# Modulation sums on TensorE: four column strips hold four column blocks over all k, and one transpose turns the rows

## The chip, the core and the metric

The kernel runs on one core of a Trainium2 chip. The metric is device time in microseconds of one execution. The core has five engines with their own instruction streams: TensorE (PE; its weight loads are listed as PEld), VectorE (DVE), ScalarE (ACT), GpSimd (POOL) and SyncE (SP, which here issues the weight transfers). They meet at semaphores only.

## The reference, cut to what matters

Two transformer blocks of 256 tokens and 1024 features. The first has two layers; each layer's norms, gates and shifts are set by a "modulation" vector, which comes from one conditioning vector for the latent stream and one for the context stream:

```python
sc, scc = jax.nn.silu(c), jax.nn.silu(c_ctx)          # c: (1, 1024), c_ctx: (1024,)
for i in range(2):
    m  = (sc  @ ada_w[i] + ada_b[i]).reshape(-1, 9, 1024)   # ada_w[i]: (1024, 9216)
    mc = (scc @ ada_w[i] + ada_b[i]).reshape(9, 1024)
    x = x + 0.5 * m[:, 2] * swiglu(modulate(x, norm_g[i, 0], m[:, 0], m[:, 1]), ...)
    ...
```

So the whole of `ada_w` (2 x 1024 x 9216 floats, 75.5 MB) is multiplied with two vectors. Everything else (five gated feed-forward layers, a state-space mixer, a pooling mixer, a second block with two mixers) is not touched by the change.

## The kernel before, in words

**Layout.** Features lie on the 128 partitions, tokens along the free axis: a stream `x` is [128, 8, 256]. A product with a weight matrix takes three TensorE passes per 128x128 block (lines 612 to 614, the helper `mm3`), because each operand is split in a high and a low part. Weights arrive in chunks of 1 MB, three slots deep: SP loads `raw`, ACT rounds it to the high part (line 1217), DVE subtracts for the low part (line 1649), and PE waits for that in `take`.

**Modulation.** The 9216 columns of a layer are taken 256 at a time: a slot `ada[i]` holds [128, 8, 256], k on partitions and in the middle index. Two slots, 512 columns, are a "pair" for this part of the kernel; there are 36 of them. The stationary operand is `scv[:, k, :]`, 128 x 32: column 0 is silu(c), column 1 silu(c_ctx), the other 30 are zero. With 32 stationary columns a matmul fills one of four column strips of the array, and writes 32 partitions of a PSUM bank.

- `ada_sums` (PE, lines 628 to 636): for each of the two slots and each k, one matmul of 256 moving columns into the strip `k % 4`. A strip thus holds the sum over two of the eight k, and the bank [128, 512] has four partial sums per column block, at rows 0, 1, 32, 33, 64, 65, 96 and 97. Operands are fp32, and each such matmul stands in the trace as two weight loads and two matmul records.
- `ada_copy` (DVE, line 1690) copies the bank to `ada_rows` in SBUF.
- `ada_turn` (PE, lines 638 to 644): four matmuls with `ada_rows` as stationary operand and the constant `strip_sum` (128 x 2) as moving operand add up the strips and put the columns on partitions: 2 results for each of 4 blocks.
- `ada_keep` (DVE, line 1695) adds the bias and stores into `mods_all`.

**Order.** Each engine's order is written out by hand. In a prologue four pairs run one after the other, sums, copy, turn, in banks 2 and 5 and with the results in bank 0; one DVE instruction (line 1778) then stores all of them. The other 32 pairs lie in the loops of the first four feed-forward layers (`ADA_LOOPS`, 10 + 10 + 10 + 2), one for each pass of `pair(j)`:

```python
hidden(g + 2, 0, None, j - 1)            # 48 passes of mm3 blocks, bank 0
ada_sums((0, 1), ..., 2)                 # bank 2
pe.wait_ge(S["h_done"], pairs + j)
down(g + 3, opens, False, j - 1)         # banks 4 to 7
ada_turn(m0 - 1 + j, 3, 0, 0)            # after a wait for mods_done; bank 3
hidden(g + 4, 1, None, j - 1)            # bank 1
```

DVE's order in the same pass: the product for `hidden`, one low part, `ada_copy`, one low part, `ada_keep`, one low part. POOL waits for `ada_done` and then issues the transfers of the next two slots (line 503), so they have almost a whole pass to land.

Of the kernel before, what the change touches and what calls it, by code (L numbers as in the profile page):

```python
# [34 lines left out]
P = 128  # L35
T = 256
TT = T // P
D = 1024
KB = D // P
# [29 lines left out]
ROT = 32  # L69
# [6 lines left out]
ADA_FIRST = 8  # L76
# [45 lines left out]
def shape_constants():  # L122
# [7 lines left out]
    causal = neg(l <= s)  # L130
# [20 lines left out]
    wide[:ROT, 2 * T + 32:] = rot  # L151
    strip_sum = (s % 32 == np.arange(2)[None, :]).astype(np.float32)
    f32 = np.concatenate([ident, mask_f, mask_b, causal, cmp_mask[0], cmp_mask[1], wide, strip_sum], 1)

# [18 lines left out]
def two_block_kernel(nc, a, out):  # L173

    ctx = ExitStack()
    with ctx:
# [20 lines left out]
        scratch = fixed("scratch", [P, KB, T])  # L197
        NCONST = P + 2 * T + P + 32 + 2 * T + 32 + ROT + 2
        consts = fixed("consts", [P, NCONST])
# [24 lines left out]
        ada += [nc.alloc_sbuf_tensor_at(f"ada{6 + i}", [P, KB, 256], F32, offset=u_at + 8 * i * KIB) for i in range(2)]  # L224
        ada_rows = [over(f"ada_rows{i}", [P, 512], (56 + 2 * i) * KIB) for i in range(2)]
        uc_hi = over("uc_hi", [P, KB, T], 16 * KIB, F32R)
# [91 lines left out]
        rot = consts[0:ROT, _o + 32:_o + 32 + ROT]  # L318
        strip_sum = consts[:, _o + 32 + ROT:_o + 34 + ROT]

# [288 lines left out]
        def _(pe):  # L609
# [18 lines left out]
            def ada_sums(slots, loads, bk):  # L628

                for n, slot in enumerate(slots):  # L630
                    pe.wait_ge(ada_in[slot], 16 * loads)
                    for k in range(KB):
                        strip = 32 * (k % 4)
                        m = pe.matmul(bank[bk][strip:strip + 32, 256 * n:256 * n + 256], scv[:, k, :],  # L634
                                      ada[slot][:, k, :], start=k < 4, stop=k >= 4)
                m.then_inc(S["ada_done"], 1)

            def ada_turn(pair, bk, at, buf):

                pe.wait_ge(S["ada_rows"], pair + 1)  # L640
                for blk in range(4):
                    m = pe.matmul(bank[bk][:, at + 2 * blk:at + 2 * blk + 2], ada_rows[buf][:, blk * P:(blk + 1) * P],  # L642
                                  strip_sum, start=True, stop=True)
                m.then_inc(S["ada_turned"], 1)

# [114 lines left out]
            for m in range(ADA_FIRST // 2):  # L760
                if m >= 2:
                    pe.wait_ge(S["ada_rows"], m - 1)
                ada_sums((2 * m, 2 * m + 1), 1, (2, 5)[m % 2])
                ada_turn(m, 0, 8 * m, m % 2)
            pe.wait_ge(S["root_done"], 2)
# [871 lines left out]
        def _(ve):  # L1637
# [49 lines left out]
            def ada_copy(pair, bk, buf):  # L1687

                ve.wait_ge(S["ada_done"], pair + 1)
                ve.tensor_copy(ada_rows[buf][:, :], bank[bk][:, :]).then_inc(S["ada_rows"], 1)  # L1690

            def ada_keep(pair):

                ve.wait_ge(S["ada_turned"], pair + 1)
                ve.tensor_tensor(mods_all[:, bass.ds(4 * pair, 4), :],
                                 bank[3][:, 0:8].rearrange("p (b v) -> p b v", v=2),
                                 cols[:, bass.ds(4 * pair, 4)].unsqueeze(2).to_broadcast([P, 4, 2]), ALU.add)\
                    .then_inc(S["mods_done"], 2)
# [74 lines left out]
            for m in range(ADA_FIRST // 2):  # L1773
                if m >= 2:
# [3 lines left out]
            ve.tensor_tensor(mods_all[:, 0:2 * ADA_FIRST, :],  # L1778
                             bank[0][:, 0:4 * ADA_FIRST].rearrange("p (b v) -> p b v", v=2),
                             cols[:, 0:2 * ADA_FIRST].unsqueeze(2).to_broadcast([P, 2 * ADA_FIRST, 2]), ALU.add)\  # L1780
# [572 lines left out]
```

## Time and profile before

| | |
|---|---|
| three executions | 2394.72, 2405.93, 2409.69 us |
| median | 2405.93 us |
| profiled execution, span from first to last instruction | 2404.9 us |
| PE busy | 2210.8 us (92%) |
| DVE busy | 1349.1 us (56%) |
| ACT busy | 989.0 us (41%) |
| POOL busy | 182.7 us (8%) |

The profiled execution's span is 1.0 us below the median of the three executions; of what lies outside the span nothing is recorded. Matmul records overlap, so a busy time of PE is not the sum of its records: where `x32` stands behind a row, the time in the row is from the first start to the last end. Read a cost on PE as the distance between the starts of its neighbours.

### The profile page before, as it was taken

To read this page: it belongs to the slowest core of one execution; us is meant where nothing else is said; L and a number is where in the kernel's file an instruction comes from. 1 tells how busy PE (TensorE), PEld (TensorE's weight loads), DVE (VectorE), ACT (ScalarE), POOL (GpSimd) and SP (SyncE) were. 2 spreads that over 40 slices of the span, in tenths; PEclk is the share of its full clock that TensorE was granted. 3 is DMA by queue.
4 is the path that set the end of the run, shared out by engine and by line. 5 is a ranking of instruction groups with operands and counts; after the bars stand their busy time and mean duration, and the time that the engine had idled before them with its cause. 6 is when DMAs were issued, how large, how long until landed. Compare 5 with 4: busy or idle time off the path is not lost.

```text
span 2404.9 us, 40229 instructions
## 1 busy us (share of the span) xinstructions
PE 2210.8 (92%) x17317; PEld 2075.3 (86%) x17317; DVE 1349.1 (56%) x1632; ACT 989.0 (41%) x1113; POOL 182.7 (8%) x153
## 2 busy tenths in 40 slices
PE   3899999989998989999999899979999898799897
PEld 2799899989977888999899899969999688799867
DVE  2544454459779965444544654455765435776543
ACT  2433354433333644333434444345444434544522
POOL 1000000000010000000000000001310000230000
PEclk7999999999998889999999999989999799899878
DMA  9477767742222436777555445535434133344401
GB/s 314 141 265 261 245 224 259 260 161 90 88 88 88 141 105 228 262 262 244 176 176 185 131 140 185 182 99 164 125 122 129 48 119 110 123 125 120 144 1 53
DMA packets 270788, 383.79 MB, mean 160 GB/s; under 512 B 8441, under 2 KB 230727, under 8 KB 270679
## 3 DMA queue, kind: packets, MB, share of 16 engines
q1 hardware_dynamic: 246983, 293.59, 38.1%
q0 software_dynamic: 22288, 85.02, 10.4%
q10 hardware_dynamic: 1408, 3.59, 0.4%
q8 instruction: 85, 1.39, 0.2%
q14 instruction: 24, 0.20, 0.0%
HBM read 381.06 MB, written 1.11 MB: 159 GB/s over the span
## 4 chain that ended last, share of the span: by engine, by line
PE 79%; DVE 13%; ACT 4%; DMA 2%; issue 2%; POOL 0%; ACTq 0%; DVEq 0%; SPq 0%
PE bank L612 22%; PE bank L613 21%; PE bank L614 21%; DVE w_hl L1649 3%; PE bank L634 3%; PE bank L986 2%; PE bank L625 2%; ACT w_hl L1217 1%; PE bank L642 1%; DVE e_long L1950 1%; DVE e_long L1968 1%; DVE rstd L1659 1%; DVE conv_acc L1899 1%; PE bank L1033 1%; DMA ada<-in_ada_w 1%
## 5 line engine op out<-in xcount | busy, mean ns | idle before, releaser
L1649 DVE TENSOR_TENSOR w_hl<-raw,w_hl 128x2048 fp32r<-128x2048 f32 (+1 forms) x281 | 640.7, 2282 | 475.5 <-ACT w_hl L1217 475.3
L612 PE MATMUL bank<-u_hi,w_hl 128*128 128x256 f32 x2376 | 696.4, 293 | 28.2 <-DVE u_lo L1680 24.4
L613 PE MATMUL bank<-u_lo,w_hl 128*128 128x256 f32 x2376 | 684.4, 288 | 0.0
L614 PE MATMUL bank<-u_hi,w_hl 128*128 128x256 f32 x2376 | 683.8, 288 | 0.0
L1217 ACT ACTIVATE w_hl<-raw 128x2048 fp32r<-128x2048 f32 (+1 forms) x281 | 531.1, 1892 | 274.8 <-PE bank L614 252.4
L612 PEld LDWEIGHTS bank<-u_hi,w_hl 128*128 128x128 f32 x2376 | 467.1, 197 | 45.0 <-issue 35.0
L613 PEld LDWEIGHTS bank<-u_lo,w_hl 128*128 128x128 f32 x2376 | 468.8, 197 | 0.5 <-issue 0.5
L614 PEld LDWEIGHTS bank<-u_hi,w_hl 128*128 128x128 f32 x2376 | 468.1, 197 | 0.0
L612 PE MATMUL bank<-h_hi,w_hl 128*128 128x256 f32 x880 | 252.2, 287 | 11.6 <-DVE h_lo L1713 11.6
L613 PE MATMUL bank<-h_lo,w_hl 128*128 128x256 f32 x880 | 248.3, 282 | 0.0
L614 PE MATMUL bank<-h_hi,w_hl 128*128 128x256 f32 x880 | 248.2, 282 | 0.0
L612 PEld LDWEIGHTS bank<-h_hi,w_hl 128*128 128x128 f32 x880 | 167.4, 190 | 25.9 <-DVE h_lo L1713 13.1
L613 PEld LDWEIGHTS bank<-h_lo,w_hl 128*128 128x128 f32 x880 | 167.4, 190 | 0.0
L614 PEld LDWEIGHTS bank<-h_hi,w_hl 128*128 128x128 f32 x880 | 167.3, 190 | 0.0
L1265 ACT ACTIVATE h_hi<-h_full 128x512 fp32r<-128x512 f32 x55 | 34.8, 632 | 296.0 <-DVE h_full L1711 296.0
L612 PE MATMUL bank<-uc_hi,w_hl 128*128 128x256 f32 x520 | 149.1, 287 | 3.6 <-DVE uc_lo L1680 2.2
L613 PE MATMUL bank<-uc_lo,w_hl 128*128 128x256 f32 x520 | 147.1, 283 | 0.0
L614 PE MATMUL bank<-uc_hi,w_hl 128*128 128x256 f32 x520 | 146.9, 282 | 0.0
L612 PE MATMUL bank<-w_hl,u_hi 128*128 128x256 f32 (+1 forms) x368 | 111.8, 304 | 16.5 <-DVE w_hl L1649 11.7
L503 POOL DMA_DIRECT2D ada<-in_ada_w x72 | 63.4, 886 | 771.0 <-PE bank L634 659.7
L613 PE MATMUL bank<-w_hl,u_hi 128*128 128x256 f32 (+1 forms) x368 | 108.7, 295 | 0.0
L614 PE MATMUL bank<-w_hl,u_lo 128*128 128x256 f32 (+1 forms) x368 | 108.5, 295 | 0.0
(333 smaller groups left out, 3437.0 us busy)
## 6 DMA issues: line engine op xcount, KB each, us to landing
ada<-in_ada_w POOLq DMA_DIRECT2D x72, 1024.0 KB, 8.2
raw<-in_w_in SPq DMA_DIRECT2D x60, 1024.0 KB, 5.2
raw<-in_ffn_w_gate SPq DMA_DIRECT2D x55, 1024.0 KB, 7.2
raw<-in_ffn_w_up SPq DMA_DIRECT2D x55, 1024.0 KB, 5.3
raw<-in_ffn_w_down SPq DMA_DIRECT2D x55, 1024.0 KB, 5.0
raw<-in_ssd_w_in SPq DMA_DIRECT2D x20, 1024.0 KB, 5.3
raw<-in_w_out SPq DMA_DIRECT2D x16, 1024.0 KB, 5.2
raw<-in_ssd_w_out SPq DMA_DIRECT2D x8, 1024.0 KB, 5.2
```

The source lines that it names most:

```text
L503: pool.dma_start(ada[slot][:, :, :], src).then_inc(ada_in[slot], 16)
L612: pe.matmul(out_, wh, xh, start=start, stop=False, skip_group_check=True)
L613: pe.matmul(out_, wh, xl, start=False, stop=False, skip_group_check=True)
L614: return pe.matmul(out_, wl, xh, start=False, stop=stop, skip_group_check=True)
L625: m = pe.matmul(bank[bk][:, 0:T], ones[:, :], scratch[:, k, :], start=k == 0, stop=k == KB - 1)
L634: m = pe.matmul(bank[bk][strip:strip + 32, 256 * n:256 * n + 256], scv[:, k, :], ada[slot][:, k, :], start=k < 4, stop=k >= 4)
L642: m = pe.matmul(bank[bk][:, at + 2 * blk:at + 2 * blk + 2], ada_rows[buf][:, blk * P:(blk + 1) * P], strip_sum, start=True, stop=True)
L986: m = pe.matmul(bank[un // 4][:, (un % 4) * P:(un % 4 + 1) * P], ka[:, h, t], qa[:, h, t], start=True, stop=True)
L1033: pe.matmul(bank[4 + hp][:, :], vsw[:, br, 0, f], pt0[:, 2 * hp:2 * hp + 2, :], start=False, stop=False, skip_group_check=True)
L1217: nc.scalar.activation(whi[slot][:, 0:n], raw[slot][:, 0:n], ACT.Copy).then_inc(S["hi_done"], 1)
L1265: nc.scalar.activation(h_hi[:, :, :].rearrange("p k t -> p (k t)"), hf[:, :], ACT.Copy)\
L1649: ve.tensor_tensor(wlo[slot][:, 0:n], raw[slot][:, 0:n], whi[slot][:, 0:n].bitcast(F32), ALU.subtract)\
```

## The change

`ada_sums` now waits for both slots, and then runs over k outside and over four blocks of 128 columns inside. Block `blk` goes to strip `blk`, and accumulates there over all eight k. The bank then holds finished sums in 128 columns: row 32 b holds block b for the latent stream, row 32 b + 1 for the context stream. The copy takes 128 columns instead of 512. `ada_turn` is one transpose of [128, 128] against the identity, after which column 32 b + v is block b, vector v; `ada_keep` and the prologue's last store read those columns with a stride of 32. The constant `strip_sum` is gone, and the turned pairs of the prologue take 128 columns of bank 0 each.

```diff
             def ada_sums(slots, loads, bk):
-                for n, slot in enumerate(slots):
+                for slot in slots:
                     pe.wait_ge(ada_in[slot], 16 * loads)
-                    for k in range(KB):
-                        strip = 32 * (k % 4)
-                        m = pe.matmul(bank[bk][strip:strip + 32, 256 * n:256 * n + 256], scv[:, k, :],
-                                      ada[slot][:, k, :], start=k < 4, stop=k >= 4)
+                for k in range(KB):
+                    for blk in range(4):
+                        strip = 32 * blk
+                        m = pe.matmul(bank[bk][strip:strip + 32, 0:P], scv[:, k, :],
+                                      ada[slots[blk // 2]][:, k, (blk % 2) * P:(blk % 2 + 1) * P],
+                                      start=k == 0, stop=k == KB - 1)
                 m.then_inc(S["ada_done"], 1)

             def ada_turn(pair, bk, at, buf):
                 pe.wait_ge(S["ada_rows"], pair + 1)
-                for blk in range(4):
-                    m = pe.matmul(bank[bk][:, at + 2 * blk:at + 2 * blk + 2], ada_rows[buf][:, blk * P:(blk + 1) * P],
-                                  strip_sum, start=True, stop=True)
-                m.then_inc(S["ada_turned"], 1)
+                pe.transpose(bank[bk][:, at:at + P], ada_rows[buf][:, :], ident).then_inc(S["ada_turned"], 1)
...
-                ada_turn(m, 0, 8 * m, m % 2)
+                ada_turn(m, 0, P * m, m % 2)
...
-                ve.tensor_copy(ada_rows[buf][:, :], bank[bk][:, :]).then_inc(S["ada_rows"], 1)
+                ve.tensor_copy(ada_rows[buf][:, :], bank[bk][:, 0:P]).then_inc(S["ada_rows"], 1)
...
-                                 bank[3][:, 0:8].rearrange("p (b v) -> p b v", v=2),
+                                 bank[3][:, 0:P].rearrange("p (b v) -> p b v", v=32)[:, :, 0:2],
...
-                             bank[0][:, 0:4 * ADA_FIRST].rearrange("p (b v) -> p b v", v=2),
+                             bank[0][:, :].rearrange("p (b v) -> p b v", v=32)[:, :, 0:2],
```

The buffer `ada_rows` shrinks from [128, 512] to [128, 128], and the table of constants by two columns.

## Rows read from the trace of the kernel before

**Rows 1.** The page: busy time, and the chain that ended last.
```profile
PE 2210.8 (92%) x17317; PEld 2075.3 (86%) x17317; DVE 1349.1 (56%) x1632; ACT 989.0 (41%) x1113; POOL 182.7 (8%) x153
...
PE 79%; DVE 13%; ACT 4%; DMA 2%; issue 2%; POOL 0%; ACTq 0%; DVEq 0%; SPq 0%
```

**Rows 2.** Windows: span, busy PE, PEld, DVE, ACT, POOL; clock, DMA share, GB/s.
```profile
380.65:400.82 20.17, 20.17 (x186) 19.11 (x185) 9.02 (x7) 9.31 (x8) 1.77 (x2) 1.00 0.78 259
1404.03:1421.18 17.15, 17.15 (x146) 17.15 (x145) 8.26 (x5) 6.75 (x6) 0.00 (x0) 1.00 0.58 189
```

**Rows 3.** TensorE's waits from 307 to 520 us: total, times, longest.
```profile
PE bank L612 <- DVE h_lo L1713: 0.4, 1, 0.4
```

**Rows 4.** The turn and the copy: ns minimum/median/maximum; who waited for them (us, times).
```profile
L642 PE MATMUL bank<-consts,ada_rows x288: 165/251/374, 57.3 to 1204.3; 128*128 128x2 f32 x144
L1690 DVE COPY ada_rows<-bank x36: 683/693/693, 56.5 to 1198.0; 128x512 f32<-128x512 f32 x36
...
  DVE mods L1695: 128.4, 31
```

**Rows 5.** The same for the sums, line 634.
```profile
L634 PE MATMUL bank<-ada,silu_c x1152: 378/379/637, 29.0 to 1197.5; 128*32 128x256 f32 x192
```

**Rows 6.** Timeline around one group of sums: start, us, engine, line.
```profile
385.37 0.28 PE L614 MATMUL bank<-u_hi,w_hl 128*128 128x256 f32 x1
...
385.58 1.93 PE L634 MATMUL bank<-ada,silu_c 128*32 128x256 f32 x32
...
387.44 0.38 PE L612 MATMUL bank<-h_hi,w_hl 128*128 128x256 f32 x1
```

**Rows 7.** Records of line 634 running in four short stretches: PE, PEld.
```profile
385.57:385.64 0.07, 0.06 (x4) 0.07 (x8) 1.00 0.00 0
385.74:385.80 0.06, 0.06 (x4) 0.00 (x0) 1.00 0.00 0
385.81:385.86 0.05, 0.05 (x8) 0.04 (x4) 1.00 0.00 0
...
386.02:386.07 0.05, 0.05 (x8) 0.04 (x4) 1.00 0.00 0
```

**Rows 8.** Timeline around one turn of the rows.
```profile
393.12 0.28 PE L614 MATMUL bank<-h_hi,w_hl 128*128 128x256 f32 x1
...
393.24 0.95 PE L642 MATMUL bank<-consts,ada_rows 128*128 128x2 f32 x8
393.44 1.91 ACT L1217 ACTIVATE w_hl<-raw 128x2048 fp32r<-128x2048 f32 x1 [5.36 <-PE bank L614]
...
394.05 0.37 PE L612 MATMUL bank<-u_hi,w_hl 128*128 128x256 f32 x1
```

**Rows 9.** Timeline around eight 128x128 transposes, line 807.
```profile
612.70 0.28 PE L614 MATMUL bank<-uc_hi,w_hl 128*128 128x256 f32 x1
612.82 1.04 PE L807 MATMUL bank<-consts,x_silu 128*128 128x128 f32 x8
613.61 0.36 PE L612 MATMUL bank<-u_hi,w_hl 128*128 128x256 f32 x1
```

**Rows 10.** The chain that ended last, in the prologue: start, us, what.
```profile
57.25 1.87 PE bank L642 x8
59.12 3.62 PE bank L634 x32
...
63.51 1.05 PE bank L642 x8
...
66.56 0.70 DVE ada_rows L1690
```

**Rows 11.** Window of the prologue, columns as in rows 2.
```profile
59.00:62.70 3.70, 3.69 (x33) 1.39 (x33) 0.00 (x0) 0.00 (x0) 0.00 (x0) 0.50 0.69 242
```

**Rows 12.** VectorE's copies from PSUM, 512 and 62 columns.
```profile
L1760 DVE COPY cols<-bank 128x512 f32<-128x512 f32 x1 | 0.7, 691 | 16.0 <-PE bank L742 16.0
...
L1761 DVE COPY cols<-bank 128x62 f32<-128x62 f32 x1 | 0.2, 211 | 0.0
```

More of the change, by code:

```diff
@@ L151, in shape_constants @@
     wide[:ROT, 2 * T + 32:] = rot
-    strip_sum = (s % 32 == np.arange(2)[None, :]).astype(np.float32)
-    f32 = np.concatenate([ident, mask_f, mask_b, causal, cmp_mask[0], cmp_mask[1], wide, strip_sum], 1)
+    f32 = np.concatenate([ident, mask_f, mask_b, causal, cmp_mask[0], cmp_mask[1], wide], 1)
     levels = np.zeros((P, len(LEVELS), P), np.float32)
@@ L197, in two_block_kernel @@
         scratch = fixed("scratch", [P, KB, T])
-        NCONST = P + 2 * T + P + 32 + 2 * T + 32 + ROT + 2
+        NCONST = P + 2 * T + P + 32 + 2 * T + 32 + ROT
         consts = fixed("consts", [P, NCONST])
@@ L224, in two_block_kernel @@
         ada += [nc.alloc_sbuf_tensor_at(f"ada{6 + i}", [P, KB, 256], F32, offset=u_at + 8 * i * KIB) for i in range(2)]
-        ada_rows = [over(f"ada_rows{i}", [P, 512], (56 + 2 * i) * KIB) for i in range(2)]
+        ada_rows = [over(f"ada_rows{i}", [P, P], (56 + 2 * i) * KIB) for i in range(2)]
         uc_hi = over("uc_hi", [P, KB, T], 16 * KIB, F32R)
@@ L318, in two_block_kernel @@
         rot = consts[0:ROT, _o + 32:_o + 32 + ROT]
-        strip_sum = consts[:, _o + 32 + ROT:_o + 34 + ROT]
         def col(name):
```

## The prediction, made before the change was run

> **What bounds the kernel now.** I read the page first: TensorE is busy for 92% of the span and makes up 79% of the chain that ended last [rows 1]. That is an average, so next I looked at the stretch that the change touches, one pass of a feed-forward loop with modulation work in it, against a pass without. TensorE is busy for the whole of both: 20.17 of 20.17 us and 17.15 of 17.15 us, at the full granted clock (1.00, which is 2.4 GHz), with VectorE at 9.02 us, ScalarE at 9.31 us and the DMA engines at 0.78 [rows 2]. The waits say the same: over some ten such passes TensorE waited 0.4 us in all [rows 3]. So in the loops each microsecond taken off TensorE's stream comes off the total, and time taken off the copies on VectorE is worth nothing. The two kinds of pass differ by 20.17 - 17.15 = 3.02 us, which is what one group of sums and one turn cost today.
>
> In the prologue it is different. Four groups run one after the other, and TensorE and VectorE take turns on the chain: turn 1.87 us, sums 3.62, copy 0.70, turn 1.05, sums, copy, and so on [rows 10]. There the copies count too.
>
> **Sums in the loops.** Now: 16 matmuls, 32 records of 256 columns. From the start of the last ordinary matmul before them to the first behind them it is 387.44 - 385.37 = 2.07 us [rows 6]. Inside, the weight loads come in rounds of four, at 385.57 (eight, the first two rounds), then four at 385.81 and four at 386.02, and none between [rows 7]: four strips stream together, a round takes about 0.215 us, and eight rounds make 1.72. The last record starts 1.93 - 0.38 = 1.55 us after the first [rows 5, 6]. After: 32 matmuls, 64 records of 128 columns, in 16 rounds. The columns streamed in each strip stay the same (8 x 256 = 16 x 128, a strip). A round of 128 fp32 columns should take half of 0.215, 0.108; the transposes of line 807, also 128 fp32 columns, are (1.04 - 0.28)/7 = 0.109 apart, with 0.28 for the length of one record, taken from their neighbour [rows 9]. I take 0.109: 16 x 0.109 = 1.744, against 1.72 now, so **+0.02 us** per group.
>
> For this the extra instructions must be free. Twice as many weight loads have to pass: four in 0.109 us. Eight ran within the first 0.07 us [rows 7], so the loading itself has room. What no row shows is twice the number of instructions fed at that rate for a whole group: 64 weight loads and 64 matmuls in 1.74 us. Between ends: the fastest that rows show is this burst (below the need, so nothing lost), and the slowest reading is that 32 pairs in 1.72 us, 0.054 us a pair, is already what the engine can be fed; then 64 pairs take 3.44, +1.72 us a group. I take the first end, since the rounds of four with gaps between them show an engine that waits for its columns, not for instructions.
>
> A rule speaks against the change here. The Trainium skill ("TensorEngine Tiling (Array Packing)", Instruction Overhead) gives each matmul an overhead of some 60 cycles and warns against taking the tiling factor from a dimension that is already small; as an estimate from that page, 32 further records at 60 cycles of 2.4 GHz, 25 ns, would add 0.8 us a group, as much as the turn gives back. The trace disagrees as far as it goes: weight loads of neighbouring strips start within hundredths of a microsecond of each other [rows 7]. It is rival B.
>
> **Turn in the loops.** Now: four matmuls, eight records, each with a weight load of 128 columns [rows 4], from 393.12 to 394.05, 0.93 us [rows 8]. After: one transpose. Eight transposes in the same kind of stream take 612.70 to 613.61, 0.91 us [rows 9]; one takes 0.91 - 7 x 0.109 = 0.14 by the same reckoning. So **-0.79 us** per turn. Bounds: nothing shows one transpose alone inside the stream; were its place as long as a whole record, 0.28, the gain would be 0.65; more than 0.93 - 0.12 (an ordinary step) = 0.81 cannot be gained.
>
> Per pass that is -0.77 us, and a pass should take 19.40. There are 36 copies in all [rows 4], of which 4 are the prologue's, so 32 passes: 32 x 0.77 = **-24.6 us**.
>
> **What could be late next there.** ScalarE waits 5.36 us for TensorE before it may round the next chunk [rows 8], so weights are ready well ahead. DMA goes from 0.78 to 0.81 at unchanged bytes. The added wait, for the second slot before the first matmul, costs nothing in the loops: POOL issues both transfers after the last group, a pass of some 20 us earlier. Behind it on TensorE stands the `down` product; it would show as a wait of line 634. VectorE's store waits for the turn (128.4 us in 31 waits [rows 4]), and the low part queued behind it is not wanted for a further two products; the turn ends earlier, so this only eases. The copy, 0.69 to about 0.28, is hidden.
>
> **Prologue.** Copies: 512 columns take 0.691 us and 62 take 0.211 [rows 12], 1.07 ns a column above a fixed part, so 128 take 0.28: -0.41 each, four times: -1.6. Turns at full clock: 1.05 [rows 10] becomes one load and one record, some 0.05 + 0.28 = 0.33: -0.72, three times: -2.2. The first turn runs at half clock, 1.87 [rows 10], and the twice as long transpose takes 0.5 to 0.66: -1.3. The sums keep their column counts: +0.02 each. Against it, the granted clock was 0.50 (1.2 GHz) in the stretch of the second group, whose sums took 3.62 us, while the third took 66.56 - 63.51 - 1.05 = 2.0 us, so at 2.4 GHz [rows 10, 11]. If the clock rises at the same moment while the work comes some 2 us earlier, half of the third group runs at the low clock: +0.9. Sum **-4.2 us**. Bounds: -5.1 without that, -1.6 if two groups run at 1.2 GHz (2 x 1.7 = 3.4 given back). Behind the prologue VectorE's norm sets the pace, and it moves up whole.
>
> **Sum.** -24.6 - 4.2 = -28.8 us: the profiled span of 2404.9 becomes 2376. The span stands 1.0 us under the median of three, 2405.93, so I forecast 2377.
>
> **Rivals.**
> *A, instructions bind (slower).* The group keeps 0.054 us a pair. +1.72 a group, times 36 = +62, less the turns and copies, 32 x 0.79 + 4.2 = 29.5: +32, **2438 us**. It decides at the point where the group grows by more than 0.79, that is where 64 pairs take over 2.5 us, 0.039 us a pair. For it: no row shows a pair faster than that over more than a few rounds. Against it: the gaps between rounds [rows 7]. The Trainium skill ("TensorE: Matmul & The Clock Gate", Wait — 56ns, not 53.3ns?) says that in one mode of decoding a matmul costs the sequencer about 62 ns; by that the group would be near 4 us, an estimate, and this case the outcome. The trace has 0.054 us a pair today, already below it. Chance 0.10.
> *B, a small part of each record is not shared.* An ordinary matmul of 256 columns steps 0.12 where its 256 streamed columns would take half of 0.215, 0.108: 0.012 over. If 32 more records each add that, a group costs +0.4 and the loops give 32 x 0.37 = 12, with the prologue's 4 less 4 x 0.4, 2.6, that is 14.5: **2391**. At 0.024 a record the loops gain nothing and the prologue 1: 2405. The row against it is that of the four loads in 0.05 us [rows 7]. The overhead that the Trainium skill names in "TensorEngine Tiling (Array Packing)" would be this case. Chance 0.12.
> *C, the loops gain nothing.* TensorE's shorter stream turns into a wait (for h, for the low part, for the slots), and only the prologue's 4 us stay: **2402**. Only 0.4 us of waiting now [rows 3] speaks against it. The same time comes out if the strips stop overlapping a little at each change of k. Chance 0.08.
> *Forecast:* 0.70.
>
> **How the numbers follow.** A measurement of this kernel tells about 1% from no change: its three executions span 15 us. Faster by over 1% means below 2381.9, 5 us above my forecast; with that scatter I give the forecast's cases 0.8 to pass it, 0.70 x 0.8 = 0.56, and a little from B: 0.58. Slower: A, 0.10. Within 1%: 0.32. The range takes in the forecast with its bounds (the prologue's -1.6, the turn's 0.65, each side's scatter of some 10 us), B and most of C: 2364 to 2402. A is left outside.
>
> **What would show it.** In the changed kernel: a pass of 19.4 us; line 634 with x64 a group, lasting 1.93 us, and weight loads in rounds every 0.11 us; the turn one record, with 0.14 us taken from its stretch; copies near 0.28 us; the prologue 4 us shorter. Wrong would be a group over 2.5 us without rounds (A), one of 2.3 us (B), or a new wait of TensorE in the passes (C).

## The result, and the profile after

The changed kernel takes **2367.44 us** (median of four executions, 2360.87 to 2368.37), beside 2403.81 us (median of four) for the kernel before: ratio 0.985, 95% interval 0.9831 to 0.9868. That is 36 us, or 1.5%, less. I had forecast 2377 us, 28.8 us less. The profiled execution has a span of 2366.4 us against 2404.9, so 38.5 us less.

The page of the kernel after, with the rows that answer to [rows 1]: 900 more records on TensorE, yet 27 us less busy time. The chain keeps its shares. This only says that nothing else took over.

```profile
PE 2183.9 (92%) x18217; PEld 2076.5 (88%) x18217; DVE 1338.3 (57%) x1632; ACT 988.8 (42%) x1113; POOL 182.7 (8%) x153
...
PE 79%; DVE 13%; ACT 4%; DMA 2%; issue 2%; POOL 0%; ACTq 0%; DVEq 0%; SPq 0%
```

**The pass.** The window of one pass with modulation work (columns as in [rows 2]): 19.40 us in place of 20.17, with TensorE busy throughout and at full clock, and no wait added. It is what the prediction named, within a hundredth. A pass without modulation work has become 0.06 us longer (17.21 between the starts of neighbouring passes, read at ScalarE's line 1262, against 17.15 in [rows 2]), which nothing in the change explains at first sight.

```profile
370.28:389.68 19.40, 19.40 (x212) 19.07 (x211) 8.72 (x8) 9.31 (x7) 1.92 (x3) 1.00 0.77 270
```

**The sums.** TensorE's timeline around one group (line 633 now, with x64; [rows 6] before): from the last ordinary matmul ahead of it to the first behind it, 387.78 - 385.68 = 2.10 us, against 2.07.

```profile
385.68 0.28 PE L612 MATMUL bank<-u_hi,w_hl 128*128 128x256 f32 x1
385.89 1.95 PE L633 MATMUL bank<-ada,silu_c 128*32 128x128 f32 x64
387.78 0.38 PE L610 MATMUL bank<-h_hi,w_hl 128*128 128x256 f32 x1
```

**The turn.** The same around one turn (line 641; [rows 8] before): one load, one record, and the next ordinary matmul starts 0.03 us behind it. From 374.06 to 374.21 is 0.15 us; from 393.12 to 394.05 it was 0.93.

```profile
374.06 0.28 PE L612 MATMUL bank<-h_hi,w_hl 128*128 128x256 f32 x1
...
374.18 0.27 PE L641 MATMUL bank<-consts,ada_rows 128*128 128x128 f32 x1
...
374.21 0.36 PE L610 MATMUL bank<-u_hi,w_hl 128*128 128x256 f32 x1
```

**The copy and who waits** (durations in ns, minimum/median/maximum, as in [rows 4]). The copy takes 292 ns in place of 693, and VectorE's wait for the turn falls from 128.4 us to 111.1. Both are hidden in the loops.

```profile
L1687 DVE COPY ada_rows<-bank x36: 283/292/293, 53.4 to 1164.0; 128x128 f32<-128x128 f32 x36
...
L641 PE MATMUL bank<-consts,ada_rows x36: 271/272/477, 53.7 to 1169.6; 128*128 128x128 f32 x36
...
  DVE mods L1692: 111.1, 31
```

**The prologue.** The chain of waits there ([rows 10] before): copy 0.30, turn 0.47 to 0.48 and then 0.33, sums 3.62, 2.27, 1.93.

```profile
53.45 0.21 DVE ada_rows L1687
...
53.70 0.47 PE bank L641
54.17 3.62 PE bank L633 x64
...
58.64 2.27 PE bank L633 x64
...
61.34 0.33 PE bank L641
61.67 1.93 PE bank L633 x64
...
64.48 0.20 DVE mods L1775
```

The third group is at both clock levels, as its window shows (0.85 on average). In the kernel before, the second group alone was at 0.50 [rows 11], and the third took 1.91 us on the chain:

```profile
58.64:60.91 2.27, 2.21 (x64) 1.90 (x64) 0.00 (x0) 0.00 (x0) 0.00 (x0) 0.85 0.03 7
```

**The sum, from the two traces.** The first copy starts at 53.36 us where it started at 56.52 [rows 4]: 3.2 us. From there to the store of the first modulations it took 15.75 us and takes 11.12: 4.6 us. 32 passes of 0.77 us: 24.6 us. That makes 32.4 of 38.5. The 3.2 us ahead of the prologue were in no step of mine, nor were the 6.1 us left over. Both are what the later experiments are about. (Against them stand the 18 passes without modulation work, 0.06 us longer each: 1.2 us.)

### The profile page after: what moved, and what is told of

Its sections match the earlier page's. It is cut to its first block, busy times and chain, and to the rows that moved or that the text cites. A ratio compares the mean times of both kernels' runs of the same rounds, so it can differ in the third digit from the quotient of the medians.

```text
span 2366.4 us, 42062 instructions
## 1 busy us (share of the span) xinstructions
PE 2183.9 (92%) x18217; PEld 2076.5 (88%) x18217; DVE 1338.3 (57%) x1632; ACT 988.8 (42%) x1113; POOL 182.7 (8%) x153
## 3 DMA queue, kind: packets, MB, share of 16 engines
q8 instruction: 87, 1.43, 0.2%
## 4 chain that ended last, share of the span: by engine, by line
PE 79%; DVE 13%; ACT 4%; DMA 2%; issue 2%; POOL 0%; ACTq 0%; DVEq 0%; SPq 0%
PE bank L610 22%; PE bank L611 21%; PE bank L612 21%; PE bank L633 3%; DVE w_hl L1646 3%; PE bank L983 3%; PE bank L623 2%; ACT w_hl L1214 1%; DVE e_long L1947 1%; DVE e_long L1965 1%; DVE rstd L1656 1%; DVE conv_acc L1896 1%; DMA raw<-in_ffn_w_up 1%; PE bank L1030 1%; DVE e_short L1950 1%
## 5 line engine op out<-in xcount | busy, mean ns | idle before, releaser
L610 PE MATMUL bank<-w_hl,u_hi 128*128 128x256 f32 (+1 forms) x368 | 111.1, 302 | 16.5 <-DVE w_hl L1646 11.7
```

The lines of the kernel that those rows point to most:

```text
L610: pe.matmul(out_, wh, xh, start=start, stop=False, skip_group_check=True)
```

## Experiments

### The two halves of the change, each without the other

**turn_four** keeps the new sums and the short copy, and turns the rows with four matmuls of two columns, as before.

```diff
-                pe.transpose(bank[bk][:, at:at + P], ada_rows[buf][:, :], ident).then_inc(S["ada_turned"], 1)
+                for blk in range(4):
+                    m = pe.matmul(bank[bk][:, at + 2 * blk:at + 2 * blk + 2], ada_rows[buf][:, :],
+                                  pick[:, 2 * blk:2 * blk + 2], start=True, stop=True)
+                m.then_inc(S["ada_turned"], 1)
...
```

The constant `pick` (128 x 8) picks the eight useful rows. It makes the table of constants longer by eight columns; that this matters shows further below.

> The sums in strips of column blocks and the copy of 128 columns as changed, but the turn again as four matmuls with eight records. If the gain of the loops is the turn (my theory), a pass with modulation work takes 20.17 + 0.02 = 20.19 us and the whole kernel about 2400 us, only the prologue's shorter copies being left. If the regrouped sums or the shorter copy carry the gain in the loops, a pass stays near 19.4 us and the whole near 2370 us.

Measured: 2404.93 us (ten executions), ratio 1.0006 (0.9994 to 1.0019). A pass takes 20.19 us. So the new sums alone gain nothing in the loops; they are the means by which the turn becomes short. In the prologue it went otherwise than either theory had it. The chain there has three times a turn of 1.86 us and a group of 3.61, one of each stands here, and the windows of the three:

```profile
68.83 1.87 PE bank L644 x8
70.70 3.61 PE bank L635 x64
```

```profile
57.07:62.55 5.48, 5.43 (x72) 4.67 (x72) 0.00 (x0) 0.00 (x0) 0.00 (x0) 0.50 0.82 286
62.92:68.39 5.47, 5.43 (x72) 4.68 (x72) 0.00 (x0) 0.00 (x0) 0.00 (x0) 0.50 0.01 3
68.83:74.31 5.48, 5.44 (x72) 4.69 (x72) 0.00 (x0) 0.00 (x0) 0.00 (x0) 0.51 0.02 3
```

All three groups and their turns ran at a granted clock of 0.50 (1.2 GHz), where in the kernel before the first of these three did [rows 10, 11] and the other two took 1.91 us each on the chain. The prologue took 19.2 us from its first copy to the store, 3.4 more than before, for work that is shorter. What engine pattern kept the clock down I can't tell from these rows. The price of a low-clock group is plain: 3.61 against 1.93.

**turn_one_matmul** turns the rows with one ordinary matmul against a constant of 8 columns, so the transpose's 128 columns are gone too.

```diff
-                pe.transpose(bank[bk][:, at:at + P], ada_rows[buf][:, :], ident).then_inc(S["ada_turned"], 1)
+                pe.matmul(bank[bk][:, at:at + 8], ada_rows[buf][:, :], pick, start=True, stop=True)\
+                    .then_inc(S["ada_turned"], 1)
...
```

> As the changed kernel, but one ordinary fp32 matmul against a 128 x 8 selector in place of the transpose: two records with two weight loads of 128 columns. If what counts is that finished sums need one turn instead of four (my theory), it costs two loads of 0.11 us and keeps most of the gain: a pass of 19.52 us, the whole about 2371 us. If the transpose's own mode is what saves, it lies near the four matmuls, a pass of about 19.8 us or more and the whole above 2380 us.

Measured: 2375.77 us (four executions), ratio 0.9893 (0.9877 to 0.991), and the pass:

```profile
370.44:389.95 19.51, 19.51 (x212) 19.18 (x212) 8.72 (x8) 9.31 (x7) 1.77 (x2) 1.00 0.80 269
```

An fp32 matmul is two records with a load of 128 columns each; the transpose is one. So one matmul in place of four gives 0.66 of the 0.77 us a pass, and the transpose gives the other 0.11. A turn takes 0.93 us of the stream with eight records, 0.26 with two and 0.15 with one. In these three forms the cost follows the number of records and not the moving columns: 8 columns in two records cost more than 128 in one. The pass came out as forecast (19.51 for 19.52), the whole 5 us above the forecast 2371, which was reckoned from the changed kernel's 2367. The eight columns of `pick` put the buffers behind the constants where they were in the kernel before, so its time should be held against that of after_old_addresses below, 2374.06, and not against 2367.

**prologue_only** puts the new sums, copy and transpose into the prologue of the kernel before, and leaves its loops alone.

```diff
...
-                ada_sums((2 * m, 2 * m + 1), 1, (2, 5)[m % 2])
-                ada_turn(m, 0, 8 * m, m % 2)
+                ada_sums_blocks((2 * m, 2 * m + 1), 1, (2, 5)[m % 2])
+                ada_turn_blocks(m, 0, P * m, m % 2)
...
```

> The changed form in the prologue's four groups alone; the 32 groups in the loops as before. Theory: the prologue is worth 4 to 5 us and the passes stay at 20.17 us, so about 2399 us; with the changed kernel's 2367 this puts 24.5 us on the loops. Rival: the changed kernel's excess over my forecast (36 instead of 29 us) lies in the prologue, whose weights also landed 3 us earlier there; then this gives 2393 us or less.

**base_again** is the kernel before, unchanged, profiled once more as a measure of what two traces of the same program differ by.

> The kernel before, unchanged, for a second trace and for the scatter. If the 3.1 us by which the first copy to ada_rows comes earlier in the changed kernel (53.4 against 56.6 us) is scatter of the transfers, this trace can have it anywhere from 53 to 57 us; if the change caused it, it stands at 56.6 us again. The time should lie within 0.5% of 2404 us.

Measured: prologue_only 2395.11 us (six executions), ratio 0.9962 (0.9949 to 0.9975), and base_again 2400.96 us (ten executions), ratio 1.0001 (0.9989 to 1.0012). The first copy of prologue_only starts at 56.58 us, like before's 56.52, and the modulations are stored 11.4 us later; in both traces of the kernel before it is 15.75 (base_again's first copy starts at 56.2 us, so it did not move either). So the prologue's share is 4.35 us by the trace. The whole lies between the theory's 2399 and the rival's 2393; by the ratio the share is 9 us, with an interval from 6 to 12. What lies beyond the 4.35 I can't place. And the earlier first copy of the changed kernel (53.36) does not come from the prologue's new code. The two traces of the same kernel before, 2404.9 and 2396.9 us, differ by 8 us: a difference of two spans is only known to that.

### Is the engine's feeding the limit of the sums?

Rivals A and B put a price on each further instruction. **pieces_64** and **pieces_32** stream the same columns in pieces of 64 and 32, so that a group has 128 and 256 pairs of load and matmul where the changed kernel has 64.

```diff
-                for k in range(KB):
-                    for blk in range(4):
+                for part in range(P // 64):
+                    for k in range(KB):
+                        for blk in range(4):
+                            strip, c = 32 * blk, 64 * part
...
```

> As the changed kernel, but each matmul of the sums streams 64 columns instead of 128: 64 matmuls and 128 pairs of load and matmul record in a group, the columns and the turn unchanged. If a group waits for its streamed columns alone, rounds of four take 0.055 us, 0.0136 us a pair, and the group stays near 1.95 us (pass 19.4 to 19.6 us, whole about 2370 us). If each pair costs something of its own, whether feeding, loading or a fixed part, it shows here first: at 0.02 us a pair the group takes 2.7 us (pass 20.2, whole 2397), at 0.027 us, the changed kernel's own pair, 3.5 us (pass 21, whole 2425).

> The same with 32 columns a matmul: 256 pairs in a group. Columns alone would still give 1.95 us a group. A floor of x us a pair gives 256 x: 3.5 us at 0.0136, 7 us at 0.027, so a pass of 21 or 24.5 us. Whatever the 64-column run leaves open (the floor lies below its need), this one shows.

Measured: pieces_64 2375.97 us (four executions), ratio 0.9886 (0.9859 to 0.9913); pieces_32 2444.62 us (one execution). TensorE's timeline around a group, first of pieces_64:

```profile
387.21 0.28 PE L612 MATMUL bank<-u_hi,w_hl 128*128 128x256 f32 x1
387.42 1.99 PE L634 MATMUL bank<-ada,silu_c 128*32 128x64 f32 x128
389.35 0.38 PE L610 MATMUL bank<-h_hi,w_hl 128*128 128x256 f32 x1
```

and of pieces_32:

```profile
383.10 0.28 PE L612 MATMUL bank<-u_hi,w_hl 128*128 128x256 f32 x1
383.31 2.36 PE L634 MATMUL bank<-ada,silu_c 128*32 128x32 f32 x256
385.60 0.39 PE L610 MATMUL bank<-h_hi,w_hl 128*128 128x256 f32 x1
```

Twice the instructions make a group 389.35 - 387.21 = 2.14 us long, against 2.10: 0.04 more. Four times make it 2.50: 0.40 more. So 64 pairs are far from the limit of the feeding: 256 pairs went through in the 2.17 us between the first and the last start, 0.0085 us a pair, where rival A had 0.054. The Trainium skill ("TensorE: Matmul & The Clock Gate", Wait — 56ns, not 53.3ns?) says that starts of matmuls never come closer than some 25 ns; for matmuls into four different strips this trace has a third of that, and the trace decides.

The whole is longer than the groups explain. The median of pieces_64 is 8.5 us above the changed kernel's, of which 36 x 0.04 explain 1.4; three of its executions took 2375 to 2377 us and the profiled one 2366.95, so no trace shows where the others lost it.

pieces_32 is 77 us slower than the changed kernel, and 36 groups x 0.40 are only 14. Most of the rest is a cost that I had in no theory. In its prologue and in the first pass or two of each loop, TensorE stands still in the middle of the group and waits for nothing that the profile shows; later passes of the same loop don't. One such place in the timeline, after 210 of 256 pairs (in brackets the idle time before the record, and what ended it):

```profile
1225.61 1.98 PE L634 MATMUL bank<-ada,silu_c 128*32 128x32 f32 x210
...
1232.74 0.86 PE L634 MATMUL bank<-ada,silu_c 128*32 128x32 f32 x46 [5.16 <-issue]
```

Twelve of the 36 groups have such gaps, 0.8 to 5.4 us each and 43 us in all; in the changed kernel and in pieces_64's loops there is none (pieces_64's prologue has two, of 1.3 and 0.7 us). That leaves 20 us; 3.3 of them lie in a stage near the end that the next section reads, and the rest I have not placed. On the page of pieces_32 the queue of kind "instruction" stands with 105 packets and 1.72 MB, on the page after with 87 and 1.43:

```profile
q8 instruction: 105, 1.72, 0.3%
```

The stalls lie where code is run for the first time, and more code is transferred. I take them for the loading of code; that was not tested by itself.

### Do the strips have to alternate?

**block_outside** has the same 64 records, in the other order of loops: one strip over all k, then the next strip.

```diff
-                for k in range(KB):
-                    for blk in range(4):
+                for blk in range(4):
+                    for k in range(KB):
```

> As the changed kernel, but the loop over the four blocks lies outside the loop over k, so that neighbouring matmuls are in the same strip. If the cheap group depends on neighbours in different strips (my theory), 64 records of 0.109 us stand one behind the other: 7.0 us a group instead of 1.95, a pass of 24.4 us, 36 x 5.0 = 180 us more, about 2550 us. If the engine overlaps what waits further back in its queue, the group stays nearer to 2 us.

Measured: 2507.42 us (one execution), with a pass of 23.39 us:

```profile
384.07 0.28 PE L612 MATMUL bank<-u_hi,w_hl 128*128 128x256 f32 x1
384.28 5.95 PE L633 MATMUL bank<-ada,silu_c 128*32 128x128 f32 x64
390.17 0.38 PE L610 MATMUL bank<-h_hi,w_hl 128*128 128x256 f32 x1
```

6.10 us a group against 2.10. Records start 0.09 us apart in place of four in some 0.11: of these two orders, the strips work side by side only in the one whose neighbours in the stream go to different strips. I had expected 5.0 us more, fully one behind another; it is 4.0. This is why the sharing is the heart of the sums. The windows of line 633 in the changed kernel show it directly (a new round in each of two stretches 0.11 us apart, with loads and matmuls of several strips at once; [rows 7] before):

```profile
385.99:386.06 0.07, 0.07 (x8) 0.07 (x12) 1.00 0.00 0
386.10:386.17 0.07, 0.07 (x12) 0.07 (x8) 1.00 0.00 0
```

### The low-clock stretches

**after_late_2** adds one more reciprocal (1.75 us) on VectorE behind the prologue of the changed kernel, to shift all that follows against the stretches of low clock.

```diff
+            ve.reciprocal(rstd[0][:, :], rms[0][:, :])
             modulation(0, 0, 1)
```

> The changed kernel with one more reciprocal of VectorE (1.75 us, repeated work, result unchanged) behind the prologue's last store. By the work alone the whole is 1.75 us longer, 2369 us. If part of the changed kernel's extra gain is where the stretches of low granted clock happen to fall, the distance will not be 1.75 us but differ by several us either way. Its first copy to ada_rows also tells whether 53.4 us (against 56.2 to 57.0 in five other traces) belongs to the changed kernel or to that one execution.

Measured: 2368.41 us (four executions), ratio 0.9857 (0.9826 to 0.9889), so 1.75 us on the chain left no mark that can be told. Its modulations were stored at 62.71 us, 1.8 before the changed kernel's 64.48, with the same code up to there: 0.8 of it is an earlier first copy (52.57), and 1.0 a shorter way from copy to store. What differs between two executions took away what I had put in.

What such stretches can do shows best where both traces have equal work. These are windows of one and the same stage near the end (377 or 378 matmul records, 59 of VectorE's instructions and 78 of ScalarE's), of the kernel before:

```profile
2233.33:2310.89 77.56, 68.45 (x378) 56.91 (x378) 38.36 (x59) 36.49 (x78) 0.00 (x0) 0.77 0.30 95
```

of base_again, which is the same program:

```profile
2228.04:2302.45 74.41, 66.34 (x378) 54.77 (x377) 38.43 (x59) 36.47 (x78) 0.00 (x0) 0.81 0.31 99
```

and of the kernel after:

```profile
2197.58:2271.76 74.18, 65.89 (x377) 54.48 (x377) 38.41 (x59) 36.46 (x78) 0.00 (x0) 0.81 0.31 100
```

So 3.4 of the 38.5 us come from a granted clock of 0.81 in place of 0.77, in a stage that the change doesn't touch, and the unchanged kernel finds 3.2 of them in another execution. The other traces show this stage at one of two lengths: with bounds at VectorE's instructions it takes 78.1 us in the kernel before, after_old_addresses, pieces_64 and pieces_32, 74.8 to 75.0 in nine others, and 77.0 in prologue_only. Both lengths are found with the new sums and the old ones, and at the old addresses and the new. So this part is not the change's. A second place is the border between the first two feed-forward layers. Windows of before, then of after; the second of each pair is the part at the low level:

```profile
285.37:313.94 28.57, 23.28 (x168) 22.46 (x168) 13.85 (x17) 13.26 (x16) 0.00 (x0) 0.94 0.53 170
302.30:305.70 3.40, 3.40 (x16) 3.40 (x17) 1.22 (x1) 2.15 (x2) 0.00 (x0) 0.50 0.55 187
```

```profile
270.17:297.12 26.95, 23.17 (x168) 22.35 (x167) 13.84 (x16) 13.26 (x16) 0.00 (x0) 0.94 0.54 186
...
277.80:281.20 3.40, 3.20 (x15) 3.20 (x16) 2.29 (x2) 3.02 (x2) 0.00 (x0) 0.50 0.00 0
```

Both have 3.4 us at the low level and nearly the same busy time of TensorE. Before, they fell behind the wait for `x_ctx`, where TensorE sets the pace; after, ahead of it, where TensorE had to wait for VectorE anyway, and the wait took them up: by the list of waits TensorE waited 3.1 us for `x_ctx` before, and 1.5 after. That is 1.6 us. The unchanged kernel finds this too: in base_again the same border is 1.5 us shorter than in the other trace of that kernel. These two places make 5.0 of the 6.1 us left over, and neither is a gain of the change.

### Where the earlier start comes from

The first copy comes 3.2 us earlier though nothing ahead of it was changed. By the chain that ended last it stands behind VectorE's low part of the second weight chunk, that behind the chunk's transfer, and that behind the sixth of the eight slots of `ada_w`, for which SyncE waits before it issues any weights. The slots' part of the chain takes 17.73 us before and 14.85 after (0.5 us more comes from `x`, which landed earlier). DMA transfers between 17 and 30 us, all of them columns of `ada_w`, of the kernel before and of the kernel after:

```profile
DMA packets 1178, 4.51 MB, mean 347 GB/s; under 512 B 78, under 2 KB 78, under 8 KB 1178
```

```profile
DMA packets 1364, 5.26 MB, mean 405 GB/s; under 512 B 79, under 2 KB 79, under 8 KB 1364
```

The same transfers run 17% faster. The change takes two columns from the table of constants, 8 bytes a partition; the kernel rounds its buffers up to 32 bytes, so every buffer behind the table moves by 32 bytes. The first six of the eight slots for `ada_w` lie there; their region now starts at 136192, a multiple of 256, in place of 136224. **after_old_addresses** is the changed kernel with two columns of zeros added to the constants.

```diff
...
-    f32 = np.concatenate([ident, mask_f, mask_b, causal, cmp_mask[0], cmp_mask[1], wide], 1)
+    f32 = np.concatenate([ident, mask_f, mask_b, causal, cmp_mask[0], cmp_mask[1], wide, np.zeros((P, 2), np.float32)], 1)
...
-        NCONST = P + 2 * T + P + 32 + 2 * T + 32 + ROT
+        NCONST = P + 2 * T + P + 32 + 2 * T + 32 + ROT + 2
...
```

> The changed kernel with two unused columns of zeros at the end of the constants, where strip_sum was. That moves every buffer behind the constants, the modulation slots among them, back by 32 bytes to the addresses of the kernel before. Theory: the slots' new addresses, not the new sums, make the first transfers faster (about 400 against 350 GB/s between 17 and 30 us); then this one has 349 GB/s, its first copy to ada_rows starts at 56.2 to 57.0 us instead of 52.6 to 53.4, and it takes 2371 us. Rival: the sums, done or arranged differently, free the transfers; then it keeps 400 GB/s, 53 us and 2367 us. The passes stay at 19.40 us either way; in the last feed-forward layer, without modulation work, a pass may return from 17.22 to 17.16 us.

Measured: 2374.06 us (five executions), ratio 0.9874 (0.9852 to 0.9897). The rate is back:

```profile
DMA packets 1188, 4.54 MB, mean 349 GB/s; under 512 B 80, under 2 KB 80, under 8 KB 1188
```

and so are the first copy, at 56.75 us, and the pass without modulation, 17.15 us. The modulations are stored at 67.39, 2.9 us later than in the kernel after. All traces agree on the rate: 347 to 349 GB/s in the six whose slots start at the old addresses (turn_four and turn_one_matmul are among them, with a table eight columns longer), and 405 to 407 in the eight with slots at a multiple of 256. So the rate goes with the slots' addresses, and neither with the sums nor with the exact size of the table.

The change proper, with the addresses as they were, is thus worth 2404.29 - 2374.06 = 30.2 us (24.8 to 35.6 by the interval); I had forecast 28.8. In its trace the prologue takes 10.64 us from copy to store, 5.1 less than before, and a pass 19.40 us, so 5.1 + 24.6 = 29.7 us are placed. Between it and the kernel after lie 6.6 us by medians, but the intervals of the two ratios overlap. Of these, the 2.9 us in the prologue go with the addresses in every trace: the first copy starts at 56.2 to 57.0 us in the six traces with the old ones, at 52.6 to 53.4 in five of those with the new ones that keep the order of the work, and at 49.8 in the sixth (pieces_32). The traces also place 3.4 in the stage near the end, which takes 77.57 us here, and 1.5 at the border between the first two layers; as said above, both come and go without the change.

The Trainium skill ("DMA: Bandwidth & Descriptors", How a descriptor splits into AXI transactions) says that transactions of at most 256 bytes start at multiples of 256 bytes. By that, as an estimate from the page, 1024 bytes (one row of a slot) that start 32 bytes beyond a multiple take five in place of four, and 4096 bytes (about what most packets hold by the counts above) 17 in place of 16. The measured ratio, 349/405 = 0.86, lies between the 0.80 and the 0.94 of these counts. No run here shows transactions, so this mechanism stays unproven.

### Versions that go further

Since the sums of a pair now take only 128 columns, four pairs fit in one bank. **one_copy** lets the prologue's four groups write to the four quarters of bank 2, copies all 512 columns at once, and then turns them with four transposes.

```diff
...
             for m in range(ADA_FIRST // 2):
-                if m >= 2:
-                    pe.wait_ge(S["ada_rows"], m - 1)
-                ada_sums((2 * m, 2 * m + 1), 1, (2, 5)[m % 2])
-                ada_turn(m, 0, P * m, m % 2)
+                ada_sums((2 * m, 2 * m + 1), 1, 2, P * m)
+            for m in range(ADA_FIRST // 2):
+                ada_turn(m, 0, P * m, 0)
...
```

> A further version: since a pair's sums now fill only 128 columns, the prologue's four groups run one after the other into the four quarters of one bank while VectorE still waits for weights; then one copy of 512 columns and four transposes. Theory: the copy starts where the first one did (53 us), the last store follows after 0.7 + 1.1 us at about 55 us instead of 64.5, and the whole is 9 us shorter, 2358 us. Rival: TensorE, longer idle before it, runs the following work at the low granted clock and gives a part back: 2361 us or more.

Measured: 2355.44 us (four executions), ratio 0.9796 (0.977 to 0.9822): 12 us less than the changed kernel. The chain of waits:

```profile
52.84 0.69 DVE ada_rows L1770
...
54.80 0.20 DVE mods L1772
```

The groups now run ahead, beside VectorE's work on the first weights. From copy to store it takes 1.96 us in place of 11.12, and the first ordinary matmul starts at 56.91 us in place of 66.59. That is 9.7 us of the 12, beside 9 forecast; the rival's loss to the low clock did not show in the whole.

The copy waits there for its place in VectorE's order, behind the low parts of two weight chunks. **one_copy_early** moves it, and the norm that uses it, ahead of them.

```diff
...
-            lo_at(0)
-            lo_at(1)
-            for m in range(ADA_FIRST // 2):
...
             apply("ctx_f0", xc, mod_a, shifted(0, 0, 1), uc_hi, uc_lo)
+            lo_at(0)
+            lo_at(1)
...
```

> As one_copy, and VectorE and ScalarE norm the context stream before they split the first two weight chunks instead of after. The last slot lands at 35 us, so sums, copy, transposes and store end at about 39 us and the norm at 46; the first chunk (landed at 43 us) is split by 50 us, and the first feed-forward layer starts there instead of at 66.6 us. Theory: 19 us shorter than the changed kernel, 2348 us. Rival: the second chunk and the other stream's norm then queue on VectorE, and little more than one_copy's gain is left: 2357 us.

Measured: 2354.92 us (four executions), ratio 0.9798 (0.977 to 0.9825), so the same as one_copy, near the rival's 2357 and not the theory's 2348. The store came 11.7 us earlier, but the first ordinary matmul waited for what had been put behind it, and started at 54.38 us, 2.5 before one_copy's. The chain, and TensorE's longest wait:

```profile
41.61 0.70 DVE ada_rows L1768
...
43.12 0.20 DVE mods L1770
...
54.38 0.55 PE bank L610
```

```profile
PE bank L610 <- DVE w_hl L1645: 11.4, 1, 11.4
```

**all_aligned** takes one_copy_early and moves all the buffers so that the slots of the ordinary weights start at multiples of 256 bytes as well.

```diff
...
-        base = 16512
+        base = 16640
...
+        top[0] += 128
         region = top[0]
...
```

> As one_copy_early, with all buffers moved so that the weight slots, too, start at multiples of 256 bytes (they were 128 off). Theory: transfers of weights also reach 400 instead of 350 GB/s; where they bind, in the first 60 us, this gives 2 to 3 us, and in the loops, where TensorE binds, nothing: 2346 us. If the speed of the modulation slots had to do with the 32 bytes only, the weights stay at 350 GB/s and the time at one_copy_early's.

Measured: 2358.0 us (four executions), ratio 0.9805 (0.9778 to 0.9831): not faster, where the theory had 2346. The weights do take less of the DMA engines' time per MB, by 8%. The hardware queue's rows between 35 and 50 us (MB, share of the time of all engines), of all_aligned and then of one_copy_early: 3.04 MB in 57.2% of the engines' time, against 3.06 MB in 62.4%.

```profile
q1 hardware_dynamic: 3019, 3.04, 57.2%
```

```profile
q1 hardware_dynamic: 3037, 3.06, 62.4%
```

But in the loops transfers are not on the path, and the pass on TensorE got longer (19.46 us, against 19.39 to 19.40):

```profile
361.47:380.93 19.46, 19.46 (x212) 19.13 (x211) 8.72 (x7) 9.32 (x7) 1.76 (x2) 1.00 0.76 270
```

one_copy and one_copy_early are the fastest; between them the runs don't decide, and one_copy is the smaller edit.

## Why the prediction was right, point by point

- **Bound.** That TensorE's stream alone sets the time in the loops held: the pass lost exactly what the stream lost, and no wait was added.
- **Sums, +0.02 us a group.** Measured 2.10 against 2.07, and 20.19 against 20.17 for the pass with the new sums and the old turn: +0.02 to +0.03. The argument from the gaps between rounds was sound, and pieces_64 shows how wide the room is: 64 more pairs for 0.04 us, 0.0006 us each where rival B had 0.012. I had given A and B 0.22 together, since no row showed more than eight loads in a burst.
- **Turn, -0.79 us.** Measured 0.15 us against 0.93, so -0.78. The reckoning from eight transposes in a row was right for one alone.
- **Copies and turns in the prologue.** Copy 0.29 against a forecast of 0.28. Turns 0.47 at the low clock and 0.33 at the full, forecast 0.5 to 0.66 and 0.33. The second turn was at the low clock too, which I hadn't counted (+0.14).
- **The third group's clock, +0.9.** The right cause and too large: 2.27 - 1.93 = 0.34. It was not even sure to come: in after_old_addresses the third group ran at full clock. The prologue gained 4.6 us in the kernel after and 5.1 in after_old_addresses, forecast 4.2. (That sum leaves out the four times 0.02 us that the same paragraph names.) turn_four shows that my bound of -1.6, with two groups at 1.2 GHz, was no bound: there three were, and the prologue lost 3.4 us. The clock's part should have been kept as a larger uncertainty.
- **Sum, -28.8.** 30.2 by medians with the addresses held (after_old_addresses), and 29.7 by its trace, so the mechanism and its size were right. The kernel after came 10 us below my figure, and its trace shows 9.7 us more than my sum. Of these, 0.4 are the prologue's. 3.2 are the earlier start, and 2.9 of them the transfers of the slots, for a cause that I had looked past: I read "the table of constants shrinks by two columns" as nothing, and the shift in addresses made these transfers 17% faster. 5.0 are where the low-clock stretches fell, which the unchanged kernel also gains or loses from one execution to the next. No step of mine held either; the room for 15 us of scatter in my range took them in, and that the measured time still lay inside is owed to that.
- **Rival C** (a new wait in the loops) did not show. DMA's busy share in the pass is 0.77, against 0.78 before, and not the 0.81 that I had. That too is the addresses': in after_old_addresses a pass has 0.81, as forecast.

What stays open: why the pass depends on addresses, what kept turn_four's clock low, what sets which of its two lengths the stage near the end takes, and where pieces_64's slower executions lost their time.

## What to carry to other kernels

Where TensorE is busy for the whole of a loop, count its records: packing the same columns into strips so that the *next* step needs one record in place of eight pays, and the additional small records cost almost nothing as long as neighbours go to different strips. A change of a buffer's size moves every buffer behind it, so before a gain is put down to an edit, run the edit with the old addresses; here 2.9 us of 36 were shown to be theirs, and by medians it may be 6.6. And differences of a few microseconds between two traces should be looked for in stages that the edit doesn't touch, with the granted clock beside them, before they are explained.

## What was not expected of the hardware

- Pairs of load and matmul of 32 columns into alternating strips went through at 0.0085 us a pair (pieces_32). The changed kernel's records of 128 columns go through at 0.027 us each in alternating strips, and at 0.09 us in one strip after another (block_outside).
- Columns of `ada_w`, in rows of 1024 bytes, went to SBUF slots at 347 to 349 GB/s where the slots start 32 bytes beyond a multiple of 256, and at 405 to 407 GB/s where they start at a multiple.
- The pass without modulation took 17.15 us in the kernel before and in after_old_addresses, 17.21 in the kernel after, and 17.28 in all_aligned, with the same instructions at a granted clock of 1.00. Only addresses differ. With modulation work, the first loop's passes took 19.28 us in the kernel after, and by turns 19.16 and 19.35 in after_old_addresses. I have no mechanism for it.
- A loop whose body has 256 short matmuls in one place stalled for up to 5.4 us in its first passes and not in later ones (pieces_32).
